# Out-projection of a hybrid mixer on one core: half the output columns in pairs of 512, with seven block products in place of eight for six of 16 tile pairs

## The chip, the core and the metric

The kernel runs on one core of a Trainium2 chip. The metric is the device time of one execution in microseconds. TensorE does matmuls of a 128x128 stationary operand with up to 512 moving columns and writes to eight banks of PSUM (128 partitions x 512 fp32). VectorE, ScalarE, GpSimd and SyncE each work through their own queue in order. Engines wait for each other through semaphores only.

## What is computed

One block of a hybrid sequence mixer, for x of 256 tokens x 4096. Cut to its frame:

```python
h = rms_norm(x, norm_g)
proj = h @ w_in                        # 256 x 4096 @ 4096 x N_IN
y_a = mLSTM heads of proj, chunked     # 1024 columns of y
y_b = sparse attention of proj         # 2048 columns
y_c = gated delta rule of proj         # 1024 columns
y = concatenate([y_a, y_b, y_c])       # 256 x 4096
out = x + y @ w_out                    # 256 x 4096 @ 4096 x 4096
```

The change is all in the last line, the out-projection. y holds 32 tiles of 128 rows of the contraction (kt 0 to 31); y_a is kt 0 to 7, y_b 8 to 23, y_c 24 to 31. Two neighbouring tiles, 2i and 2i+1, are called tile pair i here (i is 0 to 15).

## The kernel before

All weights are streamed once from HBM. The program cuts them into 536 chunks (`plan`), and every engine runs through the same list of chunks, each with its own part:

- SyncE loads chunk c into `w_raw[c % 4]`, 128 x 1024 fp32 (two tiles of the contraction x 512 columns), as soon as `w_lo` of chunk c-4 is made (`weights`).
- ScalarE writes `w_hi[c % 4]`, the same rounded to fp32r (`split_hi`, L1313), once TensorE is done with chunk c-4.
- VectorE writes `w_lo[c % 4]` = `w_raw` - `w_hi` (`split_lo`, L1650).
- TensorE (`chunk`, L1039, L1041, L1042) does three matmuls for each of two contraction tiles and two halves of the tokens: hi x hi, lo weights x hi operand, hi weights x lo operand. Twelve matmuls of 128x512 make a chunk. The operand is `op_hi` and `op_lo`, transposed tiles of h and later of y.

In the loops of ScalarE and VectorE, iteration c first handles the split of chunk c+3 (AHEAD is 3) and then the pieces woven into slot c: everything else of the mixer is cut into pieces with names of two or three letters, and `plan` writes by hand into which slot each goes. In the stretch that the change touches, these are `ae`, `ap`, `ay` (scores, product with v and norm of the mLSTM heads), `yd` and `yt` (blockwise turn of two tiles of y on VectorE, then `op_hi` on ScalarE and `op_lo` on VectorE), and `evac` (PSUM is added to x).

The out-projection is in 16 blocks. `out1` n (n from 0 to 7, chunks 408 to 503, twelve each) does kt 8 to 31 for output columns 512n and on, because y_a is not ready yet; `out2` n (chunks 504 to 535, four each) does kt 0 to 7. Both end in `evac`, which adds the two banks of 512 columns to `out_acc(n)`, first loaded with x. Even blocks use PSUM banks acc0, odd ones acc1; four more banks (mix) serve the woven pieces in turns. GpSimd loads x, moves blocks of y through HBM for the transposes and stores the finished columns. In slots 434 to 459 lie the last `ae`, `ap` and `ay`, the last `ay` in 459; `yd`/`yt` of tile pairs 0 to 3 lie in 469, 471, 473 and 475.

The order in ScalarE's and VectorE's loops:

```python
for c in range(len(chunks)):
    if c + AHEAD < len(chunks):
        split_lo(c + AHEAD)       # ScalarE: split_hi(c + AHEAD)
    for name, arg, use in woven[c]:
        pieces[name](arg, U0 + use)
```

`step(ins)` makes VectorE wait until its own instruction has ended, before it starts the next.

Of the kernel before, what the change touches and what calls it, by code (L numbers as in the profile page):

```python
# [13 lines left out]
F32 = mybir.dt.float32  # L14
# [88 lines left out]

USES = {"par": 2, "gt": 2, "gb": 1, "kx": 1, "cn": 1, "cg": 2, "cm": 1, "cu": 1,
# [4 lines left out]
def plan():  # L109
# [33 lines left out]
    for n in range(D // 512):  # L143
        block("out1", n, "y", full[kt_a:], wide, 512, "w_out", 512 * n)
    for n in range(D // 512):
        block("out2", n, "y", full[:kt_a], wide, 512, "w_out", 512 * n)

    chunks, last = [], []
    for b, blk in enumerate(blocks):
        for i in range(0, len(blk["kts"]), blk["per"]):  # L150
            chunks.append((b, blk["kts"][i:i + blk["per"]]))
        last.append(len(chunks) - 1)
# [18 lines left out]
    for b, x in enumerate(blocks):  # L171
        woven[last[b] if b else FIRST_EVAC].append(("evac", b))
# [50 lines left out]
    weave(first + 10, [("yt", i) for i in range(4, 16)])  # L223
    at = end("av", 1) + 2
# [5 lines left out]
    assert at <= end("out1", 7), (at, end("out1", 7))  # L230
# [10 lines left out]
def hybrid_kernel(nc, x, norm_g, w_in, w_out, m_ib, m_fb, m_norm_g, a_cq_g, a_wuq, a_wuqi, a_qn_g, a_kn_g,  # L241
# [13 lines left out]
    with ExitStack() as ctx:  # L255
# [6 lines left out]
        def region(names):  # L262

            with ExitStack() as stack:
# [14 lines left out]
                                       ("y_1", [P, D - 1024], F32), ("csq_lo", [P, 2, 512], F32R)])  # L279
        y = sb("y", [P, M, D])  # L280
        kv = sb("kv", [P, M, 1024])
# [7 lines left out]
        small = sb("small", [P, M, G_W])  # L289
        lane_u, lane_t = region([("lane_u", [P, BLK, LANE_C], F32), ("lane_t", [P, 320], F32)])  # L290
# [14 lines left out]

        xs, norm_in = region([("xs", [P, M, D], F32), ("norm_in", [P, P], F32)])
# [38 lines left out]
        def two_halves(v):  # L345
# [15 lines left out]
             ("a_h", [P, M, P], F32), ("a_sq", [P, P], F32), ("acc0", [P, M, W_A], F32)])  # L361

# [36 lines left out]
        rows_kept = sem("rows_kept")  # L399
        c_rows_ready = [sem(f"c_rows_ready{i}") for i in range(2)]  # L400
# [10 lines left out]
        conv_moved = [sem(f"conv_moved{i}") for i in range(2)]  # L411
# [37 lines left out]
        cq_moved = [sem(f"cq_moved{i}") for i in range(2)]  # L449
# [7 lines left out]
        bi_moved = [sem(f"bi_moved{i}") for i in range(2)]  # L457
# [5 lines left out]
        bq_moved = [sem(f"bq_moved{i}") for i in range(2)]  # L463
        bq_turned = sem("bq_turned")
        aqk_kept = sem("aqk_kept")
        aqk_moved = [sem(f"aqk_moved{i}") for i in range(2)]
# [6 lines left out]
        x_again = [sem(f"x_again{n}") for n in range(D // 512)]  # L473
        last_parts = sem("last_parts")
# [19 lines left out]

        def late_bank():
            return bank(U0 + uses)
# [157 lines left out]
        def _(sp):  # L654
# [5 lines left out]
            def weights(c):  # L660
                if c >= RAW_BUFS:
                    sp.wait_ge(lo_ready, c - RAW_BUFS + 1)
# [50 lines left out]
            for i, (m, n0, n1) in enumerate(LAST_PARTS):  # L713
                sp.wait_ge(last_out, i + 1)
                n = D - 512
# [6 lines left out]
        def _(pool):  # L722
# [68 lines left out]
            for j in range(6):  # L791
# [3 lines left out]
                bring_blocks(conv_stage(j), conv_dram[j % 2], conv_moved[j % 2])  # L795
# [108 lines left out]
            for i in range(2):  # L904
# [3 lines left out]
                bring_blocks(part, cq_dram[i], cq_moved[i])  # L908
# [6 lines left out]
            for j in range(2):  # L915
# [3 lines left out]
                bring_blocks(bi_in[j], bi_dram[j], bi_moved[j])  # L919
# [5 lines left out]
            def bring_queries(g):  # L925
# [4 lines left out]
                bring_blocks(two_halves(b_qT[:]), bq_dram[g], bq_moved[g % 2])  # L930
# [26 lines left out]
            def bring_aqk(j):  # L957

                pool.wait_ge(aqk_kept, 16 * 4 * M * (j + 1))
                bring_blocks(two_halves((a_qT, a_kT)[j][:]), aqk_dram[j], aqk_moved[j])  # L960
# [30 lines left out]
            for n in range(D // 512):  # L991
# [6 lines left out]
            for n in range(D // 512 - 1):  # L998
# [6 lines left out]
        def _(pe):  # L1005
# [6 lines left out]
            def chunk(c):  # L1012
# [3 lines left out]
                if kts[0] == blk["kts"][0] and b >= 2:  # L1016
# [5 lines left out]
                if c == len(chunks) - 1:  # L1022
                    wait_emptied(pe, U0 + uses)
# [4 lines left out]
                for i, kt, ms, n0, n1 in order:  # L1028
# [23 lines left out]
            pe_done = [0]  # L1052

# [236 lines left out]
        def _(act):  # L1290
# [906 lines left out]
```

## Time and profile before

| | us |
|---|---|
| median of 3 runs | 1540.96 |
| lowest, highest | 1540.08, 1541.07 |
| span of the profiled execution | 1538.2 |
| TensorE busy | 1533.7 |
| VectorE busy | 994.5 |
| ScalarE busy | 753.0 |
| GpSimd busy | 358.8 |

The span runs from the first to the last instruction of one profiled execution; the times of the runs also hold what lies around it. Matmuls are pipelined and the end of one is modelled, so two matmuls in a row overlap in the trace, and what one costs is read from the distance of starts. "Waited for" and "idle before" name the instruction that came last before the engine went on. PEclk is the granted clock of TensorE as a share of full speed.

### The profile page before, as it was taken

The numbers are of one execution on the slowest core, as the hardware profiler recorded it, in microseconds if no ns is written. First come the engines' busy times: TensorE is split into PE (matmuls) and PEld (weight loads), VectorE is DVE, ScalarE is ACT, GpSimd is POOL, SyncE is SP. The second block draws the span as 40 slices with busy tenths as digits, with TensorE's granted clock in tenths as the row PEclk, the third lists the DMA queues.
The fourth block names the chain that finished last, engine by engine and source line by source line (L and its number), as shares of the span: only waits on it lengthen the run. The fifth ranks groups of instructions, "written<-read, shape, count | busy, mean of one in ns | idle before, by whom it ended". The sixth has DMA issues, their size and how long they took to land.

```text
span 1538.2 us, 18847 instructions
## 1 busy us (share of the span) xinstructions
PE 1533.7 (100%) x6996; PEld 1270.8 (83%) x6996; DVE 994.5 (65%) x1537; ACT 753.0 (49%) x1006; POOL 358.8 (23%) x609
## 2 busy tenths in 40 slices
PE   9999999999999999999999999999999999999999
PEld 7888888888888888888878888888888888888887
DVE  6647555657759855676579667675456776664554
ACT  6745444587533444554545535535346444443332
POOL 9041112230230040127410354345300120200000
PEclk9999999999999999999999999999999999999999
DMA  9986778886787685568856787898885776666674
GB/s 285 292 244 196 220 213 230 204 244 190 223 242 214 196 223 159 166 182 267 250 176 194 219 244 216 228 274 249 255 250 178 249 221 192 208 198 194 196 246 156
DMA packets 206267, 337.77 MB, mean 220 GB/s; under 512 B 53049, under 2 KB 60520, under 8 KB 205920
## 3 DMA queue, kind: packets, MB, share of 16 engines
q1 hardware_dynamic: 184784, 288.66, 62.6%
q0 software_dynamic: 21344, 47.90, 11.8%
q8 instruction: 55, 0.90, 0.3%
q14 instruction: 36, 0.29, 0.1%
q10 hardware_dynamic: 48, 0.02, 0.0%
HBM read 312.81 MB, written 23.49 MB: 219 GB/s over the span
## 4 chain that ended last, share of the span: by engine, by line
PE 98%; DVE 1%; ACT 1%; issue 0%; DMA 0%; DVEq 0%
PE acc L1039 31%; PE acc L1042 31%; PE acc L1041 31%; PE mix L1102 1%; PE mix L1175 1%; PE mix L1164 0%; PE mix L1095 0%; PE acc L1243 0%; PE mix L1010 0%; DVE w_lo L1650 0%; ACT w_hi L1313 0%; PE mix L1161 0%; PE mix L1151 0%; PE mix L1149 0%; PE mix L1185 0%
## 5 line engine op out<-in xcount | busy, mean ns | idle before, releaser
L1650 DVE TENSOR_TENSOR w_lo<-w_raw,w_hi 128x1024 fp32r<-128x1024 f32 (+2 forms) x535 | 646.0, 1218 | 426.1 <-ACT w_hi L1313 422.6
L1313 ACT ACTIVATE w_hi<-w_raw 128x1024 fp32r<-128x1024 f32 (+2 forms) x535 | 556.3, 1050 | 536.3 <-PE acc L1042 434.1
L1039 PE MATMUL acc<-w_hi,op_hi 128*128 128x512 f32 (+1 forms) x2036 | 799.9, 393 | 0.3 <-DVE w_lo L1650 0.3
L1042 PE MATMUL acc<-w_hi,op_lo 128*128 128x512 f32 (+1 forms) x2036 | 792.9, 389 | 0.0
L1041 PE MATMUL acc<-w_lo,op_hi 128*128 128x512 f32 (+1 forms) x2036 | 791.9, 389 | 0.0
L1039 PEld LDWEIGHTS acc<-w_hi,op_hi 128*128 128x128 f32 x2036 | 382.5, 188 | 80.5 <-issue 1.9
L1042 PEld LDWEIGHTS acc<-w_hi,op_lo 128*128 128x128 f32 x2036 | 382.2, 188 | 80.1
L1041 PEld LDWEIGHTS acc<-w_lo,op_hi 128*128 128x128 f32 x2036 | 382.5, 188 | 77.7
L783 POOL DMA_DIRECT2D conv_dram<-y x48 | 30.7, 694 | 167.9 <-ACT y L1365 167.1
L783 POOL DMA_DIRECT2D y_dram<-y x32 | 20.5, 710 | 181.6 <-DVE y L2089 114.8
L937 POOL DMA_DIRECT2D bp_dram<-b_ps x48 | 31.5, 719 | 70.0 <-ACT b_ps L1534 67.0
L783 POOL DMA_DIRECT2D bq_dram<-qs x32 | 20.5, 715 | 76.4 <-DVE qs L1957 76.4
L1534 ACT ACTIVATE b_ps<-b_s,st 128x128 f32<-128x128 f32 (+1 forms) x32 | 14.3, 446 | 45.4 <-DVE st L2030 45.4
L948 POOL DMA_DIRECT2D b_pT<-bp_dram x48 | 26.5, 568 | 41.1 <-DMA bp_dram<-b_ps 41.0
L1039 PE MATMUL acc<-w_hi,cq_hi 128*128 128x512 f32 x84 | 33.5, 399 | 0.0
L1041 PE MATMUL acc<-w_lo,cq_hi 128*128 128x512 f32 x84 | 33.4, 397 | 0.0
L1042 PE MATMUL acc<-w_hi,cq_lo 128*128 128x512 f32 x84 | 33.1, 394 | 0.0
L789 POOL DMA_DIRECT2D y<-conv_dram x48 | 25.5, 541 | 23.5 <-DMA conv_dram<-y 23.4
L1000 POOL DMA_DIRECT2D out_dram<-acc x2 | 1.5, 729 | 125.8 <-DVE acc L1677 125.8
L1785 DVE SCALAR_TENSOR_TENSOR cT<-y,par,cT 128x255 f32<-128x255 f32 (+2 forms) x72 | 29.4, 478 | 0.0
L858 POOL DMA_DIRECT2D lane_out_dram<-lane_u x4 | 4.2, 1066 | 106.3 <-DVE lane_u L1846 106.3
L771 POOL DMA_DIRECT2D y<-in_x_dram x48 | 27.7, 585 | 0.0
(348 smaller groups left out, 974.2 us busy)
## 6 DMA issues: line engine op xcount, KB each, us to landing
w_raw<-in_w_in_dram SPq DMA_DIRECT2D x367, 512.0 KB, 4.7
w_raw<-in_w_out_dram SPq DMA_DIRECT2D x128, 512.0 KB, 4.5
w_raw<-in_w_in_dram SPq DMA_DIRECT2D x16, 384.0 KB, 3.3
w_raw<-in_a_wuq_dram SPq DMA_DIRECT2D x12, 512.0 KB, 5.4
conv_dram<-y POOLq DMA_DIRECT2D x48, 64.0 KB, 3.9
y<-conv_dram POOLq DMA_DIRECT2D x48, 64.0 KB, 4.7
w_raw<-in_a_wuqi_dram SPq DMA_DIRECT2D x6, 512.0 KB, 4.8
bp_dram<-b_ps POOLq DMA_DIRECT2D x48, 64.0 KB, 4.2
```

Source lines behind the costliest of these rows:

```text
L771: pool.dma_start(dst, src).then_inc(x_again[X_MOVED.index(c)], 16)
L783: pool.dma_start(*kept_block(dst, src, m, i)).then_inc(signal, 16)
L789: pool.dma_start(*moved_block(dst, src, q, j)).then_inc(signal, 16)
L937: pool.dma_start(bp_dram[n % 2][:, :, :, i, :].rearrange("a k j b -> a (k j) b"), b_ps[32 * i:32 * i + 32, n % 2].rearrange("p (f b) -> p ...
L948: pool.dma_start(b_pT[32 * j:32 * j + 32, n % 2], bp_dram[n % 2][:, :, j].rearrange("a k i b -> a k (i b)")).then_inc(bp_moved[n % 2], 16)
L1039: nc.tensor.matmul(o, hi[:, kt, tok], hv[:, i, n0:n1], start=(kt == (kts if late else blk["kts"])[0]), stop=False)
L1041: nc.tensor.matmul(o, hi[:, kt, tok], lv[:, i, n0:n1], start=False, stop=False)
L1042: last_mm = nc.tensor.matmul(o, lo[:, kt, tok], hv[:, i, n0:n1], start=False, stop=(kt == blk["kts"][-1]))
L1102: ins = nc.tensor.matmul(bank(use)[:, a * n:a * n + n], lhs(a), rhs(a), start=True, stop=True)
L1313: func(split_ap(w_hi, c), w_raw[:, c % RAW_BUFS, 0:n], ACT.Copy).then_inc(hi_ready, 1)
L1650: vec.tensor_tensor(split_ap(w_lo, c), w_raw[:, c % RAW_BUFS, 0:n], split_ap(w_hi, c).bitcast(F32), ALU.subtract).then_inc(lo_ready, 1)
L1785: ins = vec.scalar_tensor_tensor(cT[:, c, d:SEQ], conv_columns(i, j)[:, 0:SEQ - d], par[:, row:row + 1], cT[:, c, d:SEQ], ALU.mult, ALU.add)
```

## The change

Output columns 0 to 2047 stay as they are: `out1` and `out2` for n from 0 to 3. Columns 2048 to 4095 become two column pairs (n = 4 and 5, n = 6 and 7). A column pair goes once over all 16 tile pairs, in the order of PAIR_KTS, with the two column blocks' chunks in turn. It stands between `out1` 3 and `out2` 0: chunks 456 to 487 and 488 to 519. Four banks collect its four sums (two token halves x two column blocks): the acc banks for the first column pair, the mix banks for the second.

For tile pairs 8 to 13 (SEVEN) the 2x2 blocks of operand and of weights are multiplied by Strassen's scheme in Winograd's form, seven products in place of eight, each again of three matmuls. The chunk of the first column block (`seven_first`) has two products (6 matmuls), that of the second (`seven_second`) five (15 matmuls). Four products go to four more banks.

- Sums over y are made once: `ss` (VectorE, four operations of 128x128, then ScalarE, 512 columns rounded) and `sl` (VectorE, 512 columns), in slots 434, 437, ... 449 and 435, 438, ... 450.
- Sums over the weights are made for each of the 12 chunks of a second column block: VectorE makes `t_raw` (4 x 512) in three operations with a wait after the first and the second, within `split_lo`; ScalarE rounds it to `t_hi` (2048 columns), within `split_hi`, behind the rounding of the one raw block still wanted; VectorE makes `t_lo` (2048 columns) in `seven_lo`, which stands behind `split_lo` of the next chunk. There is one buffer of each.
- In the order of chunks a seven takes two, and two plain chunks lie between two sevens; in the first column pair the second chunks of the sevens are 461, 465, 469, 473, 477 and 481. Of `seven_second`'s five products the first reads only raw weights' splits, the other four read `t_hi` and `t_lo`.
- `evs` recombines the four banks of the Strassen products into the sums with x (one ScalarE copy, eight VectorE operations), behind the last seven of a column pair; `evn` adds the four plain banks at its end.
- `w_raw` of a first chunk is kept until the sums of the second are made. Some semaphores are merged into `brought` to stay within their number. Loads of x and stores of out move in GpSimd's queue.

```diff
+OUT_SINGLE = 4
+PAIR_KTS = [14, 15, 8, 4, 9, 5, 10, 6, 11, 7, 12, 0, 13, 1, 2, 3]
+SEVEN = [8, 9, 10, 11, 12, 13]
...
+    for n in range(OUT_SINGLE, D // 512):
+        block("pair", n, "y", [2 * i + j for i in PAIR_KTS for j in range(2)], wide, 512, "w_out", 512 * n)
...
+    weave(first + 26, [("ss", i) for i in SEVEN], 3)
+    weave(first + 27, [("sl", i) for i in SEVEN], 3)
...
             def weights(c):
                 if c >= RAW_BUFS:
-                    sp.wait_ge(lo_ready, c - RAW_BUFS + 1)
+                    d = c - RAW_BUFS
+                    sp.wait_ge(lo_ready, d + 2 if in_seven(d) and not second_col(d) else d + 1)
...
+            def three(o, x_hi, x_lo, w_hi_, w_lo_, start, stop):
+                nc.tensor.matmul(o, x_hi, w_hi_, start=start, stop=False)
+                nc.tensor.matmul(o, x_hi, w_lo_, start=False, stop=False)
+                return nc.tensor.matmul(o, x_lo, w_hi_, start=False, stop=stop)
...
+            def seven_first(c):
...
+                three(seven_banks(p)[0], op_hi[:, 2 * i, tok], op_lo[:, 2 * i, tok], hv[:, 0], lv[:, 0],
+                      i == SEVEN[0], i == SEVEN[-1])
+                three(plain_banks(p)[0], op_hi[:, 2 * i + 1, tok], op_lo[:, 2 * i + 1, tok], hv[:, 1], lv[:, 1],
+                      False, False).then_inc(split_used, 1)
...
+            def seven_second(c):
...
+                pe.wait_ge(lo_ready, c + 1)
...
+                three(c12, *s4, hv[:, 1], lv[:, 1], False, False)
+                pe.wait_ge(t_lo_ready, sevens.index(c) + 1)
+                three(c21, *a22, t_hi[:, 3], t_lo[:, 3], False, False)
+                three(p5, *s1, t_hi[:, 0], t_lo[:, 0], first, end_)
+                three(p6, *s2, t_hi[:, 2], t_lo[:, 2], first, end_)
+                three(p7, *s3, t_hi[:, 1], t_lo[:, 1], first, end_).then_inc(split_used, 1)
...
             def split_hi(c):
                 act.wait_ge(raw_ready[c % RAW_BUFS], raw_count(c))
                 if c >= SPLIT_BUFS:
...
+                    wait_used(act, c - SPLIT_BUFS)
...
+                if in_seven(c) and second_col(c):
+                    func(w_hi[:, c % SPLIT_BUFS, 512:1024], w_raw[:, c % RAW_BUFS, 512:1024], ACT.Copy
+                         ).then_inc(hi_ready, 1)
+                    act.wait_ge(t_summed, sevens.index(c) + 1)
+                    if c > sevens[0]:
+                        wait_used(act, sevens[sevens.index(c) - 1])
+                    func(t_hi[:], t_raw[:], ACT.Copy).then_inc(t_hi_ready, 1)
+                    return
...
             def split_lo(c):
                 dve.wait_ge(hi_ready, c + 1)
+                if in_seven(c) and second_col(c):
...
+                    step(vec.tensor_tensor(t_raw[:, 0:2], w_raw[:, b0 + 1].rearrange("p (k n) -> p k n", k=2),
+                                           w_raw[:, b0:b0 + 2, 0:512], ALU.subtract))
+                    step(vec.tensor_tensor(t_raw[:, 2], b22, t_raw[:, 0], ALU.subtract))
+                    vec.tensor_tensor(t_raw[:, 3], w_raw[:, b0, 512:1024], t_raw[:, 2], ALU.subtract
+                                      ).then_inc(t_summed, 1)
+                    vec.tensor_tensor(w_lo[:, c % SPLIT_BUFS, 512:1024], b22,
+                                      w_hi[:, c % SPLIT_BUFS, 512:1024].bitcast(F32), ALU.subtract
+                                      ).then_inc(lo_ready, 1)
+                    return
...
+            def seven_lo(c):
+
+                n = sevens.index(c)
+                dve.wait_ge(t_hi_ready, n + 1)
+                vec.tensor_tensor(t_lo[:], t_raw[:], t_hi[:].bitcast(F32), ALU.subtract).then_inc(t_lo_ready, 1)
...
+            def ss(i, use):
+                a11, a21, a12, a22 = [y_columns(i)[:, P * j:P * j + P] for j in range(4)]
+                step(vec.tensor_tensor(a22, a21, a22, ALU.add))
+                step(vec.tensor_tensor(a21, a11, a21, ALU.subtract))
+                step(vec.tensor_tensor(a11, a22, a11, ALU.subtract))
+                vec.tensor_tensor(a12, a12, a11, ALU.subtract).then_inc(s_summed, 1)
...
                 if c + AHEAD < len(chunks):
                     split_lo(c + AHEAD)
+                if c + AHEAD - 1 in sevens:
+                    seven_lo(c + AHEAD - 1)
```

## Rows read from the trace of the kernel before

**Rows 1.** The page: span, busy time of each engine, chain that ended last by engine.
```profile
span 1538.2 us, 18847 instructions
...
PE 1533.7 (100%) x6996; PEld 1270.8 (83%) x6996; DVE 994.5 (65%) x1537; ACT 753.0 (49%) x1006; POOL 358.8 (23%) x609
...
PE 98%; DVE 1%; ACT 1%; issue 0%; DMA 0%; DVEq 0%
```
**Rows 2.** What TensorE waited for: line, releaser, us in total, times, longest.
```profile
PE mix L1250 <- DVE kv L2139: 1.1, 1, 1.1
PE acc L1039 <- DVE w_lo L1650: 0.3, 1, 0.3
```
**Rows 3.** Timeline, two chunks of an `out1` block: start, duration, engine, instruction, idle before.
```profile
1401.79 0.39 PE L1042 MATMUL acc<-w_hi,op_lo 128*128 128x512 f32 x1
...
1402.01 0.39 PE L1039 MATMUL acc<-w_hi,op_hi 128*128 128x512 f32 x1
...
1402.27 1.06 ACT L1313 ACTIVATE w_hi<-w_raw 128x1024 fp32r<-128x1024 f32 x1 [1.66 <-PE acc L1042]
...
1403.37 1.23 DVE L1650 TENSOR_TENSOR w_lo<-w_raw,w_hi 128x1024 fp32r<-128x1024 f32 x1 [1.49 <-ACT w_hi L1313]
...
1404.73 0.39 PE L1039 MATMUL acc<-w_hi,op_hi 128*128 128x512 f32 x1
```
**Rows 4.** Groups by shape, whole run: the splits of 1024 columns (busy us, mean ns).
```profile
L1650 DVE TENSOR_TENSOR w_lo<-w_raw,w_hi 128x1024 fp32r<-128x1024 f32 x513 | 623.1, 1225 | 405.9 <-ACT w_hi L1313 402.6
L1313 ACT ACTIVATE w_hi<-w_raw 128x1024 fp32r<-128x1024 f32 x513 | 536.8, 1056 | 523.5 <-PE acc L1042 429.7 <-DMA w_raw<-in_w_in_dram 85.9 <-DMA w_raw<-in_w_out_dram 7.4
```
**Rows 5.** Groups by shape, whole run: 512 columns on VectorE and ScalarE.
```profile
L1361 ACT ACTIVATE qs<-acc 128x512 f32<-128x512 f32 x10 | 6.0, 597 | 1.4 <-PE acc L1042 1.0 <-issue 0.2
L1650 DVE TENSOR_TENSOR w_lo<-w_raw,w_hi 128x512 fp32r<-128x512 f32 x6 | 4.1, 689 | 4.0 <-ACT w_hi L1313 3.8
L1313 ACT ACTIVATE w_hi<-w_raw 128x512 fp32r<-128x512 f32 x6 | 3.7, 622 | 0.0
```
**Rows 6.** Timeline near 1309 us: two splits back to back on an engine.
```profile
1308.54 1.99 ACT L1313 ACTIVATE w_hi<-w_raw 128x1024 fp32r<-128x1024 f32 x2
...
1309.62 2.36 DVE L1650 TENSOR_TENSOR w_lo<-w_raw,w_hi 128x1024 fp32r<-128x1024 f32 x2 [1.85 <-ACT w_hi L1313]
```
**Rows 7.** Timeline near 10 us: TensorE starts again behind VectorE.
```profile
9.20 0.88 DVE L2131 SCALAR_TENSOR_TENSOR op_lo<-mix,par,op_hi 128x256 fp32r<-128x256 f32 x2 [1.43 <-ACT op_hi L1579]
...
10.23 0.30 PEld L1243 LDWEIGHTS acc<-w_hi,op_hi 128*128 128x128 f32 x2 [0.35 <-DVE op_lo L2131]
10.26 0.47 PE L1243 MATMUL acc<-w_hi,op_hi 128*128 128x512 f32 x1
```
**Rows 8.** DMA issues: count, KB each, median us from issue to landing.
```profile
w_raw<-in_w_out_dram SPq DMA_DIRECT2D x128, 512.0 KB, 4.5
```
**Rows 9.** VectorE's timeline: first instruction of an `ay` and the split behind it.
```profile
1290.44 0.16 DVE L1696 TENSOR_SCALAR st<-st 128x2 f32<-128x2 f32 x1
...
1293.26 1.22 DVE L1650 TENSOR_TENSOR w_lo<-w_raw,w_hi 128x1024 fp32r<-128x1024 f32 x1
```
**Rows 10.** Groups by shape, whole run: `yd`, `yt` on both engines, a 128-wide operation.
```profile
L2098 DVE STREAM_TRANSPOSE y<-y 128x512 f32<-128x512 f32 x16 | 11.3, 704 | 0.0
L1564 ACT ACTIVATE op_hi<-y,par 128x256 fp32r<-128x256 f32 x16 | 7.2, 498 | 7.7 <-DVE y L2098 7.7
L2110 DVE SCALAR_TENSOR_TENSOR op_lo<-y,par,op_hi 128x256 fp32r<-128x256 f32 x16 | 7.0, 479 | 3.9 <-ACT op_hi L1564 3.9
...
L2014 DVE TENSOR_TENSOR sc<-sc,low 128x128 f32<-128x128 f32 x2 | 0.6, 292 | 0.1
```
**Rows 11.** Busy us by stretch: PE, PEld, DVE, ACT, POOL; PEclk, DMA share, GB/s.
```profile
1255.00:1300.00 45.00, 45.00 (x212) 36.81 (x211) 32.04 (x67) 19.85 (x31) 9.40 (x16) 1.00 0.68 209
20.00:1538.00 1518.00, 1515.20 (x6912) 1255.54 (x6910) 983.05 (x1519) 741.41 (x987) 340.73 (x565) 1.00 0.75 218
```

More of the change, by code:

```diff
@@ L149, in plan @@
     for b, blk in enumerate(blocks):
+        second = blk["kind"] == "pair" and blk["arg"] % 2
+        if second:
+            last.append(len(chunks) - 1)
+            last[b - 1] = last[b] - 1
+            continue
         for i in range(0, len(blk["kts"]), blk["per"]):
-            chunks.append((b, blk["kts"][i:i + blk["per"]]))
+            for q in range(2 if blk["kind"] == "pair" else 1):
+                chunks.append((b + q, blk["kts"][i:i + blk["per"]]))
         last.append(len(chunks) - 1)
@@ L171, in plan @@
     for b, x in enumerate(blocks):
-        woven[last[b] if b else FIRST_EVAC].append(("evac", b))
+        if x["kind"] != "pair":
+            woven[last[b] if b else FIRST_EVAC].append(("evac", b))
+        elif x["arg"] % 2:
+            of_seven = [c for c, (b_, kts) in enumerate(chunks) if b_ == b and kts[0] // 2 in SEVEN]
+            woven[of_seven[-1]].append(("evs", x["arg"] // 2 - OUT_SINGLE // 2))
+            woven[last[b]].append(("evn", x["arg"] // 2 - OUT_SINGLE // 2))
     woven[NX - 1].append(("par", 0))
@@ L229, in plan @@
     at = weave(at + 8, [[("yd", i), ("yt", i)] for i in range(4)], 2)
-    assert at <= end("out1", 7), (at, end("out1", 7))
+    first_a = next(c for c, (b, kts) in enumerate(chunks) if blocks[b]["kind"] == "pair" and kts[0] == 0)
+    assert at <= first_a, (at, first_a)
     use, order = 0, {}
@@ new lines, in seven_second @@
+            def seven_second(c):
+                p, i = pair_of(c), chunks[c][1][0] // 2
+                pe.wait_ge(lo_ready, c + 1)
+                hv = split_ap(w_hi, c).rearrange("p (k n) -> p k n", k=2)
+                lv = split_ap(w_lo, c).rearrange("p (k n) -> p k n", k=2)
+                s2, s3, s4, s1 = [(s_hi(i)[:, P * j:P * j + P], s_lo(i)[:, P * j:P * j + P]) for j in range(4)]
+                tok = slice(P, 2 * P)
+                a22 = op_hi[:, 2 * i + 1, tok], op_lo[:, 2 * i + 1, tok]
+                _, p5, p6, p7 = seven_banks(p)
+                _, c21, c12, _ = plain_banks(p)
+                first, end_ = i == SEVEN[0], i == SEVEN[-1]
+                three(c12, *s4, hv[:, 1], lv[:, 1], False, False)
[4 more added lines that the diff above has]
+                three(p7, *s3, t_hi[:, 1], t_lo[:, 1], first, end_).then_inc(split_used, 1)
@@ new lines, in evn @@
+            def evn(p, use):
+                b = pair_block(p)
+                for k in range(4):
+                    if k % 2 == 0:
+                        dve.wait_ge(acc_ready, b + 1 + k // 2)
+                    dst = pair_sum(p)[:, k % 2, 512 * (k // 2):512 * (k // 2) + 512]
+                    ins = vec.tensor_tensor(dst, plain_banks(p)[k], dst, ALU.add)
+                    if p == 1:
+                        done_bank(ins, four_mix(1)[k])
+                    elif k % 2:
+                        ins.then_inc(acc_read[k // 2], 1)
+                    else:
+                        step(ins)
```

196 lines of the change are left out of this document (163 added, 33 removed).

## The prediction

> **What bounds the kernel now.** The page comes first [rows 1]: TensorE is busy in 1533.7 of 1538.2 us and 98% of the chain that ended last is TensorE's, nearly all of it in the three matmul lines of `chunk`. The list of what TensorE waited for is a few rows, 1.1 us the longest [rows 2]. So every matmul lies on the path, and the other engines count only where they make TensorE wait. A chunk is twelve 128x512 matmuls; the timeline [rows 3] has the same point of two neighbouring chunks at 1402.01 and 1404.73, so a chunk takes 2.72 us and a matmul 0.227 us (the 0.39 us shown for one overlap the next). VectorE with 65% and ScalarE with 49% look as if they had room. Those are averages; what matters below is how long a chain across them takes.
>
> How that chain stands today is in the same rows. Let T be the moment at which TensorE goes on from chunk d to d+1 (1402.01). ScalarE starts `w_hi` of chunk d+4 at T + 0.26 (the buffer of d is free), VectorE starts its `w_lo` 1.10 us later, at T + 1.36, and is done at T + 2.59. TensorE wants it at T + 3 x 2.72 = T + 8.16. The slack is 5.6 us per chunk. It is this that the change spends.
>
> **What is removed.** For each of six tile pairs in each of two column pairs, 24 matmuls become 21 (seven products of three, where eight were): 12 x 3 = 36 matmuls, 36 x 0.227 = 8.2 us off the path. There is no other removal; the chunks stay 536, and the bytes of weights the same. "Seven" below is such a tile pair; its chunks are s-1 (first column block, 6 matmuls, 1.36 us) and s (second, 15 matmuls, 3.40 us). Between two sevens lie two plain chunks, so the period is four chunks, 10.88 us today and 45 x 0.227 = 10.20 us if nothing waits.
>
> **What is added at each seven, step by step.** At s the four weight sums have to be made, split into high and low, and only then can twelve of its fifteen matmuls run (the first three need only the raw block). Durations: ScalarE takes 1.06 us for 1024 columns and 0.62 for 512 [rows 4, 5], 0.43 us more for 512 more, so 1.93 for `t_hi` (2048). VectorE takes 1.22 for 1024 and 0.69 for 512 [rows 4, 5], so 2.30 for `t_lo`. Between engines 0.04 us pass, from TensorE's last matmul 0.09 [rows 3]; two operations back to back on one engine overlap by some 0.1 us, their pairs taking 1.99 and 2.36 us [rows 6]. With T the end of chunk s-4:
> - ScalarE: `w_hi` of s, 512 columns, T+0.26 to 0.88.
> - VectorE: the sum over 1024 columns to 2.14, then the two over 512, each waiting for the one before: to 3.60. Nothing overlaps here, because each `step` waits.
> - ScalarE: `t_hi`, 3.64 to 5.57. It sits inside `split_hi(s)`, so what is queued behind it is `w_hi` of chunk s+1: in place of T+2.98 it starts at 5.44 and ends at 6.50.
> - VectorE: in its order `split_lo(s+1)` stands ahead of `seven_lo(s)`. So `w_lo` of s+1 runs from 6.54, and `t_lo` from 7.67 to 9.97.
> - TensorE: two plain chunks and s-1 take it to T+6.80, its first three matmuls of s to 7.48. Then it waits for `t_lo`. After a wait the first weight load starts 0.15 us and the first matmul 0.18 us after the releaser, and that matmul takes 0.08 longer [rows 7]: 10.23. Twelve matmuls more: 12.95.
>
> The wait is 2.75 us, and as s is the s-4 of the next seven, this is a closed loop: 12.95 us in place of 10.88, **2.07 us lost per seven** after the matmuls saved. The first seven of a column pair starts from the same T with the same chain. Twelve times: **+24.8 us**. Bounds: with no hop at all and `t_lo` at 2 us the wait would be some 2.1 us (+17 us in sum); with every hop doubled and half a microsecond of delay of `w_hi` of s+1 it is 3.5 (+34).
>
> Does anything else bind in the loop? Weights: the buffer of s-1 is now kept until the sums are made, so two transfers are issued at about T+4.3; a transfer lands in 4.5 us [rows 8], the second some 2 us later, at 9 and 11. They are wanted at T+7.06 and T+13.2, and TensorE only comes to the first of them behind the wait. Nothing is added. VectorE's work in a period is 1.2 + 1.2 + 1.2 for the three full splits, 2.6 for sums, 0.6 and 2.2, together 9.0 of 12.95 us: it fits, and there would be room even in 10.2.
>
> **Pieces that share the queues.** In the first column pair four pieces `yd`/`yt` and one `ay` are woven among the sevens. Where one stands behind `t_lo` or behind the split of s+3, VectorE comes late to the next sums, which it could start at T+13.87 (0.92 behind 12.95). `ay` takes 2.82 us, from 1290.44 to the next split at 1293.26 [rows 9]: 9.97 + 2.82 + two splits of 1.13 and 1.23 = 15.1, +1.2. A `yd`/`yt` is a turn of 0.70 on VectorE, two `op_hi` of about 0.9 on ScalarE and two `op_lo` of about 0.9 on VectorE, one after another [rows 10]: 2.5 us. The first comes behind a split at 12.2, giving +0.9; the second and third fall into one loop (9.97 + 2.5 + 2.4 + 2.5 = 17.3), +3.4; the fourth +1.0. Sum **+6.5 us**, bounds 0 (all in idle time) and 12 (each in full).
>
> **Sums over y.** Six `ss` and six `sl` are put between chunks 434 and 450, each some 1.3 us (four 128-wide operations of 0.29 and their waits) and 0.7 us of VectorE [rows 5, 10]: 12 us. In the 45 us from 1255 to 1300 it has 32.0 us of work already [rows 11], so it comes to 44 of 45, with an order in which ScalarE and VectorE wait for each other twice per `ss`. The slack of 5.6 us takes most of it; at the `ae` of chunk 448, counting on from the evacuation at 443, the splits of 452 and 453 come some 0.5 and 1.4 us late. I take **+2 us**, bounds 0 and 6.
>
> **At no cost.** The Strassen products are evacuated by one ScalarE copy (0.60 [rows 5]) and eight VectorE operations of 0.6 to 0.73: behind the last seven's end they take VectorE from 0.90 to 6.2, the next split is done at 7.5, TensorE wants it at 8.16. The cover is three plain chunks; without them up to 5 us would show, twice. `evn` (four operations, 2.9 us) has the cover of `evac`. Loads of x and stores of out move on GpSimd's queue into the middle of the run; 0.5 MB lands in 4 to 5 us [rows 8] and nobody comes for it sooner. Merged semaphores change no wait's time. The tail is the same code.
>
> **Sum.** The times shown are 1540.08 to 1541.07, median 1540.96; the profiled span is 1538.2, 2.8 us less, and I let those 2.8 us stand. 1540.96 + 24.8 + 6.5 + 2 = 1574.3 us.
>
> **Rivals.**
> - *The chain is hidden and the saving stands.* 1540.96 - 8.2 = 1532.8. For it: 65% and 49% busy engines, 5.6 us of slack. Against it: `t_lo` would have to be there at T+7.48, 2.5 us sooner than rows of these very lines allow. It takes a faster pass over 2048 columns than any row shows, or an order that isn't the code's. 0.09.
> - *The chain shows only in part*, net near nothing: 0.03. The turning point is a wait of 0.68 us per seven.
> - *Only the loop costs*; y's sums and the woven pieces fall into idle time: 1540.96 + 24.8 = 1565.8. 0.25.
> - *The forecast*, 1574.3: 0.45.
> - *The pieces cost more*, each in full, with late weights besides: 24.8 + 12 + 6 and some 6 more, about 1590. 0.12.
> - *The clock falls behind the waits.* The granted clock is 1.00 in every stretch, which is 2.4 GHz [rows 11], but TensorE never waits longer than 1.1 us there [rows 2], so no row tells what 2.75 us would do. At half the clock (1.2 GHz) the twelve matmuls behind each wait take 2.72 us more: 1574.3 + 12 x 2.72 = 1607. 0.06. [...]
> - *The change doesn't do what it says.* The code issues 21 matmuls per seven; the count has to fall from 6996 to 6960. I give this nothing of its own.
>
> **How the numbers follow.** The likeliest case gives 1574.3. The range reaches from 1558 (the loop's lower bound with nothing more) to 1594 (pieces in full) and holds the three middle cases, 0.82. What a measurement can tell from no change is about 0.2%, 3 us. Faster 0.09, within 0.2% 0.03, slower 0.88.
>
> **What would show it.** 6960 matmuls. TensorE waiting twelve times on the line of `t_lo`, some 2.7 us each and 33 in sum, longer (4 to 6 us) at two or three places in the first column pair, and hardly there on `w_lo`. ScalarE's `w_hi` of s+1 starting at once behind `t_hi`, VectorE idle between `w_lo` of s and of s+1. Distance between ends of sevens near 12.95 in the second column pair. A few microseconds of waits on `w_lo` between chunks 448 and 454. What would make it wrong: a 2048-wide operation at another price per column, weights landing late now that two start together, or the clock.

## The result and the profile after

| | before | after |
|---|---|---|
| median | 1541.01 us (1540.08 to 1541.35, 4 runs) | 1585.86 us (1583.7 to 1589.02, 4 runs) |
| ratio | | 1.0292, 95% interval 1.028 to 1.0304 |
| span of the profiled execution | 1538.2 | 1587.3 |

The change makes the kernel 44.9 us slower. The profiled execution of the changed kernel is the slowest of its four (1589.0 us, with a mean granted clock of 0.989 where the others have 0.991 or 0.992), so its trace shows 3 us more than the median, and sums read from it are held against the trace.

A remark on the text ahead of the prediction: it puts the sums over y (`ss`, `sl`) into slots 434 to 450. That is 16 slots too late; `first` in `plan` is 392, not 408, and they stand in 418 to 434, from 1211 to 1255 us in the trace of after. The load of VectorE there (1210 to 1255 us of the old trace) is 32.5 of 45 us, much as the 32.0 of [rows 11].

The page of the changed kernel, the lines that answer to [rows 1]:
```profile
span 1587.3 us, 18905 instructions
...
PE 1546.2 (97%) x6960; PEld 1274.4 (80%) x6960; DVE 1056.0 (67%) x1623; ACT 772.6 (49%) x1026; POOL 357.7 (23%) x609
...
PE 86%; DVE 8%; ACT 3%; issue 2%; DMA 1%; ACTq 0%; DVEq 0%
```
The matmuls are down by 36, as promised, and TensorE is busy for 12.5 us longer all the same: some of its matmuls have become slower. 14% of the chain that ended last is not TensorE's now (8% VectorE, 3% ScalarE, the rest issue and DMA). What TensorE waits for, where [rows 2] had 1.4 us:
```profile
PE acc L1179 <- DVE t_lo L1850: 17.8, 6, 4.2
PE mix L1179 <- DVE t_lo L1850: 14.3, 6, 2.6
PE acc L1163 <- DVE w_lo L1843: 4.4, 5, 1.8
```
Twelve waits for `t_lo`, one per seven ("acc" is the first column pair, "mix" the second), and four new ones for `w_lo` (4.1 us; the fifth of the row stands before the change's stretch), all between 1226 and 1259 us, where the sums over y stand.

What those sums cost in all is read from matmuls that are the same in both kernels, number 5601 and number 5761 of TensorE's, around that stretch. Before, then after:
```profile
1225.51 0.39 PE L1039 MATMUL acc<-w_hi,op_hi 128*128 128x512 f32 x1
1259.70 0.40 PE L1042 MATMUL acc<-w_hi,op_lo 128*128 128x512 f32 x1
```
```profile
1224.75 0.39 PE L1163 MATMUL acc<-w_hi,op_hi 128*128 128x512 f32 x1
...
1242.36 0.50 PE L1163 MATMUL acc<-w_hi,op_hi 128*128 128x512 f32 x1 [1.85 <-DVE w_lo L1843]
...
1266.46 0.40 PE L1166 MATMUL acc<-w_hi,op_lo 128*128 128x512 f32 x1
```
34.2 us have become 41.7: 7.5 us lost here, more than the waits alone show, because restarts and one stretch of slow matmuls (below) come on top.

The first seven of the second column pair, all engines (start, duration, instruction, idle before):
```profile
1441.09 0.63 ACT L1478 ACTIVATE w_hi<-w_raw 128x512 fp32r<-128x512 f32 x1 [1.94 <-PE mix L1166]
...
1441.75 1.23 DVE L1833 TENSOR_TENSOR t_raw<-w_raw 128x1024 f32<-128x1024 f32 x1 [1.34 <-ACT w_hi L1478]
1443.01 0.69 DVE L1835 TENSOR_TENSOR t_raw<-w_raw,t_raw 128x512 f32<-128x512 f32 x1
1443.74 0.69 DVE L1836 TENSOR_TENSOR t_raw<-w_raw,t_raw 128x512 f32<-128x512 f32 x1
...
1444.46 1.92 ACT L1483 ACTIVATE t_hi<-t_raw 128x2048 fp32r<-128x2048 f32 x1 [2.74 <-DVE t_raw L1836]
1446.29 1.99 ACT L1485 ACTIVATE w_hi<-w_raw 128x1024 fp32r<-128x1024 f32 x2
...
1447.36 1.23 DVE L1843 TENSOR_TENSOR w_lo<-w_raw,w_hi 128x1024 fp32r<-128x1024 f32 x1 [2.33 <-ACT w_hi L1485]
1448.50 2.28 DVE L1850 TENSOR_TENSOR t_lo<-t_raw,t_hi 128x2048 fp32r<-128x2048 f32 x1
...
1450.84 0.50 PE L1179 MATMUL mix<-t_hi,op_hi 128*128 128x512 f32 x1 [2.65 <-DVE t_lo L1850]
...
1452.30 0.63 PE L1181 MATMUL acc<-t_hi,s_even 128*128 128x512 f32 x1
...
1455.28 0.39 PE L1163 MATMUL mix<-w_hi,op_hi 128*128 128x512 f32 x1
```
Counted back 0.26 us from ScalarE's start, as in the prediction, T is 1440.83, and `t_lo` ends at 1450.78, T + 9.95. (TensorE itself went on at 1440.55; ScalarE came 0.28 us late to this first seven. In the next one TensorE goes on at 1455.28 and the first product with t starts at 1465.29, 10.01 us later, as in all loops after it.) ScalarE starts `w_hi` of the next chunk right behind `t_hi`, and VectorE sits idle for 2.33 us before that chunk's `w_lo`, which stands ahead of `t_lo`. Then comes what the chain of steps doesn't explain: from the fifth matmul behind the wait on, eight stand 0.42 or 0.43 us apart and not 0.227, and the twelve take 4.44 us. The same stretch by windows (PE, PEld, DVE, ACT, POOL; then granted clock, DMA share, GB/s):
```profile
1441.00:1447.00 6.00, 6.00 (x28) 4.98 (x27) 3.21 (x4) 3.17 (x3) 0.00 (x0) 1.00 0.47 145
1448.30:1450.80 2.50, 0.00 (x0) 0.00 (x0) 2.50 (x3) 1.06 (x1) 0.00 (x0) 1.00 0.84 271
1451.90:1455.20 3.30, 3.30 (x9) 2.61 (x8) 1.16 (x2) 0.00 (x0) 0.00 (x0) 0.50 0.56 159
1455.40:1461.00 5.60, 5.60 (x27) 4.58 (x26) 3.21 (x4) 2.72 (x3) 0.00 (x0) 1.00 0.08 14
```
The granted clock is 0.50 (1.2 GHz) for the stretch behind the wait and back at 1.00 after it. The trace has ten such stretches of seven or eight slow matmuls: nine behind waits for `t_lo`, one behind the wait of 1.85 us for `w_lo` at 1242 us. They don't follow every wait: behind those at 1340.88 (3.38 us idle), 1479.74 (2.35) and 1507.10 (2.33) the matmuls run at full clock.

### The profile page after: what moved, and what is told of

Read it like the earlier page. It is cut to its first block, busy times and chain, and to the rows that moved or that the text cites. A ratio compares the mean times of both kernels' runs of the same rounds, so it can differ in the third digit from the quotient of the medians.

```text
span 1587.3 us, 18905 instructions
## 1 busy us (share of the span) xinstructions
PE 1546.2 (97%) x6960; PEld 1274.4 (80%) x6960; DVE 1056.0 (67%) x1623; ACT 772.6 (49%) x1026; POOL 357.7 (23%) x609
## 3 DMA queue, kind: packets, MB, share of 16 engines
q0 software_dynamic: 21344, 47.90, 11.3%
## 4 chain that ended last, share of the span: by engine, by line
PE 86%; DVE 8%; ACT 3%; issue 2%; DMA 1%; ACTq 0%; DVEq 0%
PE acc L1163 26%; PE acc L1166 25%; PE acc L1165 25%; DVE w_lo L1843 3%; ACT w_hi L1485 2%; DVE t_lo L1850 2%; PE mix L1271 1%; DVE t_raw L1833 1%; PE mix L1344 1%; DMA w_raw<-in_w_out_dram 1%; PE mix L1163 1%; PE mix L1165 1%; PE mix L1166 1%; PE mix L1179 1%; PE acc L1179 1%
## 5 line engine op out<-in xcount | busy, mean ns | idle before, releaser
L1163 PE MATMUL acc<-w_hi,op_hi 128*128 128x512 f32 (+1 forms) x1860 | 733.0, 394 | 4.5 <-DVE w_lo L1843 4.4
L1166 PE MATMUL acc<-w_hi,op_lo 128*128 128x512 f32 (+1 forms) x1860 | 724.6, 390 | 0.0
L1165 PE MATMUL acc<-w_lo,op_hi 128*128 128x512 f32 (+1 forms) x1860 | 724.3, 389 | 0.0
L1163 PEld LDWEIGHTS acc<-w_hi,op_hi 128*128 128x128 f32 x1860 | 349.9, 188 | 79.1 <-DVE w_lo L1843 7.1
L1166 PEld LDWEIGHTS acc<-w_hi,op_lo 128*128 128x128 f32 x1860 | 349.5, 188 | 74.2
L1165 PEld LDWEIGHTS acc<-w_lo,op_hi 128*128 128x128 f32 x1860 | 349.9, 188 | 71.0
L1483 ACT ACTIVATE t_hi<-t_raw 128x2048 fp32r<-128x2048 f32 x12 | 23.0, 1918 | 34.9 <-DVE t_raw L1836 34.9
L1706 ACT ACTIVATE b_ps<-b_s,st 128x128 f32<-128x128 f32 (+1 forms) x32 | 14.3, 446 | 45.8 <-DVE st L2290 45.8
L1163 PE MATMUL mix<-w_hi,op_hi 128*128 128x512 f32 (+1 forms) x82 | 31.8, 387 | 0.0
L1166 PE MATMUL mix<-w_hi,op_lo 128*128 128x512 f32 (+1 forms) x82 | 31.8, 387 | 0.0
L1165 PE MATMUL mix<-w_lo,op_hi 128*128 128x512 f32 (+1 forms) x82 | 31.7, 387 | 0.0
```

Source lines behind the costliest of these rows:

```text
L1163: nc.tensor.matmul(o, hi[:, kt, tok], hv[:, i, n0:n1], start=(kt == (kts if late else blk["kts"])[0]), stop=False)
L1165: nc.tensor.matmul(o, hi[:, kt, tok], lv[:, i, n0:n1], start=False, stop=False)
L1166: last_mm = nc.tensor.matmul(o, lo[:, kt, tok], hv[:, i, n0:n1], start=False, stop=(kt == blk["kts"][-1]))
L1483: func(t_hi[:], t_raw[:], ACT.Copy).then_inc(t_hi_ready, 1)
```

## The experiments

Theory A, as in the prediction with what the trace added: a chain of dependent steps makes TensorE wait at each seven, and behind such a wait the clock often falls. Theory B: VectorE simply has too much work there. Theory C: products that read `t_hi` and `t_lo` are slow of themselves.

### One line moved: `t_lo` ahead of the next split

```diff
-                if c + AHEAD < len(chunks):
-                    split_lo(c + AHEAD)
                 if c + AHEAD - 1 in sevens:
                     seven_lo(c + AHEAD - 1)
+                if c + AHEAD < len(chunks):
+                    split_lo(c + AHEAD)
```


> One change to the changed kernel: in VectorE's loop seven_lo(s) stands ahead of split_lo(s+1), not behind it. Same instructions, same bytes. Theory A (the wait is a chain of dependent steps, and the clock falls behind the waits): t_lo needn't wait for w_hi and w_lo of chunk s+1 any more and ends 2.1 us sooner, at T+7.9 where the changed kernel has T+9.95 (T is the end of chunk s-4). TensorE's twelve waits on t_lo fall from 32.1 us in sum to 5 to 10, the stretches at 1.2 GHz behind them become fewer than the nine there are; time about 1551 us (1544 to 1560). Theory B (VectorE has too much work in the column pairs, 9.0 us in 10.2): order alone changes nothing in the sum of work, the time stays at 1580 or more. Theory C (the four products read t_hi and t_lo slowly, whatever comes before): the waits go but the slow matmuls stay, 7 or 8 of them in nine sevens: about 1565.

Measured: 1558.19 us (1557.97 to 1559.51), ratio 1.0111 (1.0095 to 1.0127). The time lies within what was expected (1544 to 1560), above its middle of 1551. Two statements in another order are worth 27.7 us. What TensorE waited for:
```profile
PE acc L1179 <- DVE t_lo L1850: 9.8, 6, 2.7
PE acc L1163 <- DVE w_lo L1843: 3.9, 4, 1.8
PE acc L1179 <- DVE w_lo L1838: 2.2, 2, 1.8
PE mix L1179 <- DVE t_lo L1850: 1.9, 6, 0.6
```
In the second column pair 14.3 us of waits are 1.9, a loop takes 10.84 us, and no slow stretch is left there. Products that read t stand 0.233 us apart where the others have 0.227, not 0.43, so theory C falls as an account of the slow stretches. The first column pair keeps 12.0 us and two slow stretches, and the waits sum to 13.9 us where 5 to 10 were expected: there the order of the chain isn't all.

### The sums over weights one chunk sooner

```diff
             def split_lo(c):
                 dve.wait_ge(hi_ready, c + 1)
                 if in_seven(c) and second_col(c):
-                    ... three sums into t_raw
...
+                    seven_lo(c)
                     return
...
+            def seven_sums(c):
+                dve.wait_ge(raw_ready[c % RAW_BUFS], raw_count(c))
+                if c > sevens[0]:
+                    dve.wait_ge(t_lo_ready, sevens.index(c))
+                ... the same three sums
...
                 if c + AHEAD < len(chunks):
                     split_lo(c + AHEAD)
-                if c + AHEAD - 1 in sevens:
-                    seven_lo(c + AHEAD - 1)
+                if c + AHEAD + 1 in sevens:
+                    seven_sums(c + AHEAD + 1)
```


> One change to the changed kernel: the three sums over weights are made one chunk sooner, behind split_lo(s-1), as soon as the raw weights are there, and t_hi then only waits for TensorE's end of chunk s-4; t_lo stands behind w_lo of s, ahead of the next split. Same instructions, same bytes. Theory A: t_hi runs from T+0.8 to T+2.7, t_lo to T+5.1, 2.4 us before TensorE wants it at T+7.5. No waits on t_lo, at most one or two where pieces are woven in, no slow stretch in the column pairs; the 8.2 us of the 36 matmuls show, and what is left is the stretch of the sums over y (4.1 us of waits on w_lo and one slow stretch): 1541 - 8.2 + 7 = 1540 us (1535 to 1546), against 1586 of the changed kernel. Theory B (too much work for VectorE): 1575 or more, with waits on w_lo or t_lo all along the column pairs. Theory C: slow matmuls stay in the sevens, 1555.

Measured: 1553.88 us (1552.73 to 1555.08), ratio 1.0081 (1.0066 to 1.0097). Expected were 1535 to 1546, so this missed by some 8 us. In the second column pair nothing waits any more, and sevens follow each other every 10.30 us. In the first one the waits stayed, two slow stretches among them:
```profile
PE acc L1179 <- DVE t_lo L1858: 8.9, 5, 2.5
PE acc L1163 <- DVE w_lo L1838: 5.6, 6, 1.8
PE acc L1179 <- DVE w_lo L1832: 1.3, 2, 1.0
```
VectorE between two sevens of the first column pair, with one `yd`/`yt` behind the sums and one behind a split:
```profile
1368.63 0.69 DVE L1850 TENSOR_TENSOR t_raw<-w_raw,t_raw 128x512 f32<-128x512 f32 x1
1369.36 0.69 DVE L1851 TENSOR_TENSOR t_raw<-w_raw,t_raw 128x512 f32<-128x512 f32 x1
1369.97 0.70 DVE L2366 STREAM_TRANSPOSE y<-y 128x512 f32<-128x512 f32 x1
1371.65 0.88 DVE L2378 SCALAR_TENSOR_TENSOR op_lo<-y,par,op_hi 128x256 fp32r<-128x256 f32 x2 [0.98 <-ACT op_hi L1736]
1372.45 0.68 DVE L1832 TENSOR_TENSOR w_lo<-w_raw,w_hi 128x512 fp32r<-128x512 f32 x1
1373.97 2.29 DVE L1858 TENSOR_TENSOR t_lo<-t_raw,t_hi 128x2048 fp32r<-128x2048 f32 x1 [0.84 <-ACT t_hi L1483]
```
Here theory B has a part, but not all of it. A loop holds about 9 us of VectorE's work and has 10.3 us; with the pieces, this one (1365.2 to 1380.7) holds 11.5 us, more than a loop of 10.3 has room for. But it took 15.5 us, and VectorE stood idle in 4.0 of them, nearly all of it for ScalarE: 1.1 us for a `w_hi`, 0.98 us for `op_hi`, twice, and 0.84 us for `t_hi`, which ScalarE started only behind the first of these `op_hi` and the `w_hi` of 512 columns. So a piece costs its own work and also lengthens the chain, because it stands ahead of `t_hi` in ScalarE's queue and ahead of `w_lo` and `t_lo` in VectorE's. No run here separates the two.

### Zero products in the wait

```diff
+FILL = 10
...
+            step(nc.gpsimd.memset(zeros[:].bitcast(F32), 0.0))
...
                 three(c12, *s4, hv[:, 1], lv[:, 1], False, False)
+                pe.wait_ge(const_ready, 2)
+                for _ in range(FILL):
+                    nc.tensor.matmul(c12, zeros[:], hv[:, 1], start=False, stop=False)
                 pe.wait_ge(t_lo_ready, sevens.index(c) + 1)
```


> The changed kernel with ten more matmuls of 128x512 per seven, put in front of TensorE's wait for t_lo: a zero operand times w_hi, added into a sum, so 2.27 us of matmuls without effect in a wait of 2.3 to 4.2 us. 120 matmuls more. Theory A with the clock as a cause of its own: t_lo comes as late as before, so TensorE goes on at the same points of the chain, but the clock has no reason to fall; the waits on t_lo shrink to 5 to 12 us in sum, the nine slow stretches in the column pairs go or nearly, each worth 8 matmuls x 0.2 = 1.6 us: 1586 - 14 = 1572 us (1568 to 1577), faster with more matmuls. Theory C (the products with t_hi and t_lo are slow of themselves): slow stretches stay, time 1586. If TensorE's order costs more than thought: 1590 or more.

Measured: 1578.61 us (1576.9 to 1580.6), ratio 1.0242 (1.0226 to 1.0258): 7.3 us faster than the changed kernel, with 120 matmuls more (expected 1568 to 1577, so the gain was smaller than forecast). `t_lo` comes when it came, and TensorE goes on at the same point of the loop, but the clock holds:
```profile
1458.99 2.43 PE L1222 MATMUL mix<-w_hi,zeros 128*128 128x512 f32 x10
1461.50 0.50 PE L1182 MATMUL mix<-t_hi,op_hi 128*128 128x512 f32 x1
1461.83 0.40 PE L1183 MATMUL mix<-t_lo,op_hi 128*128 128x512 f32 x1
```
One slow stretch is left of ten. In the second column pair the first product with t starts every 12.91 or 12.92 us in all five intervals, where the changed kernel has 14.45, 14.45, 12.91, 14.45 and 12.92. So a slow stretch costs 1.53 us there. In the first column pair it may cost nothing: the interval from 1383.58 to 1399.91 of the changed kernel is 16.33 us with a slow stretch in it, and the one of this kernel is 16.33 without: VectorE is what comes last there. And where the clock holds in the stretch of the sums over y, TensorE runs ahead and waits longer (5.6 us on `w_lo` in place of 4.4): between the same two matmuls 7.4 us are lost here and 7.5 in the changed kernel, so the slow stretch cost nothing there. That is why it is 7.3 us and not the 14 I had expected: ten times 1.6 was too simple a sum.

### The sums made only once

```diff
-                pe.wait_ge(t_lo_ready, sevens.index(c) + 1)
+                pe.wait_ge(t_lo_ready, 1)
...
-                    act.wait_ge(t_summed, sevens.index(c) + 1)
                     if c > sevens[0]:
-                        wait_used(act, sevens[sevens.index(c) - 1])
+                        return
+                    act.wait_ge(t_summed, 1)
                     func(t_hi[:], t_raw[:], ACT.Copy).then_inc(t_hi_ready, 1)
...
+                    if c > sevens[0]:
+                        ... w_lo of the raw block alone
+                        return
...
-                if c + AHEAD - 1 in sevens:
+                if c + AHEAD - 1 == sevens[0]:
```


> The changed kernel with t_raw, t_hi and t_lo made for the first seven only; the other eleven multiply with that old t. Left out: eleven times the three sums, the rounding and the split of t (output differs for that reason). TensorE's instructions are all there, 36 fewer than before. It measures the saving by itself. Theory A: one wait on t_lo (3.4 us and a slow stretch), the sums over y as before (4.1 us of waits and one slow stretch of 1.6): 1541 - 8.2 + 3.5 + 4.1 + 2 x 1.6 + restarts of 1 = 1545 us (1540 to 1549). Theory B: the same or less. Theory C: the products read t tiles that nobody writes; if reading from there is slow, slow matmuls stay in the sevens and it is 1560. If the order of blocks and banks in pairs costs by itself, it shows here as what is above 1549.

Measured: 1544.36 us (1543.24 to 1544.98), ratio 1.0021 (1.0011 to 1.0031), as expected (1545). Where no t is made there is no wait, and a loop takes 10.30 us. From it the saving is read: 10.88 - 10.30 = 0.58 us per seven, 7.0 us in all, where I had 0.68 and 8.2. Most of the missing 0.10 us shows in the distances of starts: the twelve products that read `t_hi` or `t_lo` stand 0.233 us apart, here and in every other kernel with sevens, and all others 0.227, which makes 0.08 us per seven. Why these are 3% slower no run tells.

### Seven products in the second column pair only

```diff
-            return blocks[b]["kind"] == "pair" and kts[0] // 2 in SEVEN
+            return blocks[b]["kind"] == "pair" and blocks[b]["arg"] >= 6 and kts[0] // 2 in SEVEN
...
-    weave(first + 26, [("ss", i) for i in SEVEN], 3)
-    weave(first + 27, [("sl", i) for i in SEVEN], 3)
+    for i, at in zip(SEVEN, SUM_AT):       # SUM_AT = [68, 70, 72, 74, 85, 87]
+        weave(first + at, [("ss", i), ("sl", i)])
```
with the order of the second experiment; the first column pair runs plainly.

> The order of e2 (sums over weights one chunk sooner), with seven products only in the second column pair; the first takes all its tile pairs plainly. The six sums over y are made in slots 460, 462, 464, 466, 477 and 479, where no piece of the mixer is left but yd/yt in 469 to 475, in place of 418 to 434 among the pieces of the heads. 18 matmuls fewer than before the change, 18 x 0.227 = 4.1 us. Theory A (VectorE's and ScalarE's queue decide where a seven can be had for nothing: in e2 the second column pair shows no wait at all, all 16 us of waits are where other pieces are woven in): no wait of TensorE on t_lo or w_lo, no stretch at 1.2 GHz, 1540.9 - 4.1 = 1536.8 us (1535.5 to 1539), faster than the kernel before. Theory B (a column pair costs something by itself, in banks, loads of x or stores): 1541 or more with no wait in the trace that explains it.

Measured: 1536.32 us (1534.48 to 1537.21), ratio 0.9972 (0.9962 to 0.9982). It is faster than both kernels, by 3.9 us against the one before (1540.22 in the same runs), and within what was expected. The profile lists no wait of TensorE behind 976 us; its longest ones, all up to there:
```profile
PE mix L1420 <- DVE kv L2411: 1.1, 1, 1.1
PE mix L1331 <- issue: 0.4, 1, 0.4
PE acc L1391 <- ACT w_hi L1780: 0.4, 1, 0.4
```
So neither the column pairs nor their banks, loads and stores cost anything that shows, and between the two matmuls around 1225 and 1260 us, where the sums over y have been taken away, nothing is lost (0.05 us).

### The sums over y spread out

The second experiment with `ss` and `sl` in slots 423, 426, 436, 439, 444 and 452, each `sl` one behind.

```diff
-    weave(first + 26, [("ss", i) for i in SEVEN], 3)
-    weave(first + 27, [("sl", i) for i in SEVEN], 3)
+    for i, at in zip(SEVEN, SUM_AT):       # SUM_AT = [31, 34, 44, 47, 52, 60]
+        weave(first + at, [("ss", i), ("sl", i)])
```


> e2 with the six sums over y (ss and sl) spread over slots 423 to 452, into slots where no other piece stands, in place of every third slot from 418 on. All else as e2, whose TensorE waits 4.9 us on w_lo between 1230 and 1260 us. Theory A (local backlog on VectorE, and ScalarE and VectorE waiting for each other): these waits go, the waits of the first column pair stay at about 10 us; e2's 1553.9 - 5 - 0.5 = 1548 us (1546 to 1550.5). Theory B (VectorE is full over the whole stretch of the heads, so that spreading only moves the waits): 1552 to 1555.

Measured: 1551.66 us (1551.33 to 1553.37), ratio 1.0076 (1.0061 to 1.0092). 2.2 us less than the second experiment, between the two theories:
```profile
PE acc L1180 <- DVE t_lo L1859: 8.1, 4, 2.5
PE acc L1164 <- DVE y L1930: 2.3, 1, 2.3
PE acc L1180 <- DVE w_lo L1833: 1.8, 1, 1.8
PE acc L1164 <- DVE w_lo L1839: 1.4, 2, 1.1
```
The waits at 1230 to 1260 us are gone, but one of 1.1 us stands at 1293 and one of 2.3 us at 1323, behind VectorE's late `evac`. Spread out, the same work still isn't free among the heads' pieces (4.4 us are lost ahead of the first seven, where the second experiment lost 6.6); in the experiment above, behind the heads, it costs nothing.

### The chain alone, and filled

The faster kernel (seven products in the second column pair only), with the changed kernel's order of sums, `t_hi` and `t_lo` put back (the second experiment's diff taken back); and the same with ten zero products ahead of each wait.

> e5 (seven products in the second column pair only, sums over y in free slots) with the order of the changed kernel put back: sums within split_lo(s), t_hi behind them, t_lo behind split_lo(s+1). The chain is the only thing that differs from e5, and no other piece is woven there. Theory A: six loops of 12.92 us where e5 has 10.20, so 6 x 2.72 = 16.3 us of waiting, and the clock falls behind some four of six waits as it did in the changed kernel's second column pair, 1.53 us each (a loop of 14.45 in place of 12.92): 1536.3 + 16.3 + 6.1 = 1559 us (1556 to 1562). If the chain's price depends on what else is woven in (theory B), the waits come out other than 2.3 us each and the time below 1552 or above 1565.

> e8 with ten matmuls of a zero operand ahead of each of the six waits on t_lo, 60 more in all, as in e3. It measures the clock's share alone: the loops stay at 12.92 us because t_lo comes when it comes, and no stretch at 1.2 GHz is left. Theory A with the clock as a second cause: e8 less 1.53 us for each of its slow loops, 1552.8 us (1551 to 1555), 3 to 9 us below e8. If the slow stretches were of no account (TensorE would wait for VectorE all the same): the same time as e8.

Measured: 1554.26 us (1553.44 to 1555.16), ratio 1.0087 (1.0073 to 1.0101); filled 1551.46 us (1550.56 to 1552.19), ratio 1.007 (1.0056 to 1.0084). The chain alone:
```profile
PE mix L1181 <- DVE t_lo L1851: 14.1, 6, 2.4
...
1431.51 0.50 PE L1181 MATMUL mix<-t_hi,op_hi 128*128 128x512 f32 x1 [2.35 <-DVE t_lo L1851]
...
1444.43 0.79 PE L1181 MATMUL mix<-t_hi,op_hi 128*128 128x512 f32 x1 [2.33 <-DVE t_lo L1851]
...
1458.73 0.50 PE L1181 MATMUL mix<-t_hi,op_hi 128*128 128x512 f32 x1 [2.33 <-DVE t_lo L1851]
```
The loops are 12.92 us, and 14.30 and 14.34 where the clock falls (the row of 0.79 us is a slow matmul). 1554.26 lies below the expected 1556 to 1562. Of the 4.7 us to its middle 3.3 are the clock, which fell behind two of six waits and not behind four, and 0.6 are the loops without the chain, which take 10.30 us and not 10.20. Filled, it came within what was expected, and all five intervals are 12.91 or 12.92. So the chain costs 6 x (12.92 - 10.30) = 15.7 us for six sevens (expected 16.3); the medians give 1551.46 - 1536.32 = 15.1. The clock costs another 2.8 for two stretches. Waits of one length and one spacing had four slow stretches behind them in the changed kernel's second column pair and two here: how many come can't be told from the waits.

## Why the prediction was right, and which step was not

I forecast 1574.3 us in 1558 to 1594 and slower with 0.88. It is 1585.9. The sign and the main cause hold; one cause I had put aside is in the result, and one term was far too small. The terms are read from the traces. In that of the changed kernel the last matmul starts 49.05 us later than before, though at 1225 us, ahead of all that was changed, it was 0.8 us early by chance; what was added behind is 49.8. In the kernel with zero products, where the clock holds but for one stretch, the last matmul is 40.65 us late, and 0.6 of it by chance. The profiled executions are 2 to 3 us above the medians of their kernels, so the terms don't add up to 44.9.

- **The loop.** Forecast 12.95 us, `t_lo` ended at T+9.97, a wait of 2.75. Measured 12.92 and T+9.95, and the first product with t starts 2.53 us later than it could (T+10.01 for T+7.48); the idle time of 2.33 us in the list counts from the modelled end of the last matmul. The 2048-wide steps, which no row showed, took 1.92 and 2.28 us against 1.93 and 2.30. Two small errors cancel: the restart costs 0.17 us and not 0.26, and the twelve products with t take 2.80 and not 2.72. 12 x (12.92 - 10.88) = 24.5 us, forecast 24.8. The mechanism is right; one line moved undoes most of it.
- **The saving.** 7.0 us and not 8.2, but the sum above compares loops and is not touched by it.
- **Pieces in the first column pair.** Forecast 6.5, measured 6.6 with the clock held (zero products), in part by luck. There the intervals of the first column pair are 14.03, 12.92, 13.70, 16.33 and 14.46 us, the last with a slow stretch of about 1.5. Above 12.92 that is 1.1 for `ay` (forecast 1.2), then 0, then 0.8 and 3.4 for `yd`/`yt` (forecast 0.9 and 3.4), and 0 for the fourth (forecast 1.0). The other 1.3 are at a place that I had put at nothing, "the same T with the same chain": the first seven of the first column pair came 1.0 us late, because the last `ap`, woven into slot 456, keeps ScalarE until 1329.7 us, so that `w_hi` and `w_lo` of chunk 460, behind which the sums stand, come late (with no piece there, in the chain alone, `t_lo` of the first seven ends at T+9.96 like the others); the first of the second column pair came 0.3 late, and why is open.
- **Sums over y.** Forecast 2 with bounds of 0 and 6, at a place that was 16 slots off. Measured 7.5 us between the two matmuls around them, 7.4 with the clock held, and nothing when the sums stand behind the heads. This term of the sum was mis-sized, and outside its bounds: four waits of 0.3 to 1.85 us, with their restarts, are in it where I had counted splits that come 0.5 and 1.4 us late at one place and a slack that takes most of it.
- **The clock.** This is the step that failed. I left it out of the sum and gave it 0.06 as a rival. It fell ten times. 24.5 + 6.6 + 7.4 makes 38.5 us; of the 49.8 us 11.3 are left, and these are the clock's, all in the column pairs. The run with zero products bears it out: 38.5, its one slow stretch of 1.5 and the 0.6 make 40.6 of its 40.65. My price for the rival, twelve matmuls at half the clock behind each wait (+32.6 us, 1607), was wrong too: 7 or 8 matmuls are slow, 1.4 to 1.5 us, and only where nothing else is late. I argued that no row showed a wait of this length, and took that for a reason to leave it out; it was a reason to put one end of the range there. That the range held the time it owes to the width given for the pieces: without the clock, 38.5 us would have given about 1579. The Trainium skill, TensorE: Matmul & The Clock Gate, section "Why this matters for your kernels", has the rule that idle gaps between bursts of matmuls, beyond a length that it names, send the array to half rate. The trace agrees as to the fall and not as to the length: eight of the ten falls stand behind waits shorter than the page's (1.85 to 2.65 us), and behind one of 3.38 us, which is longer, there was none.
- **At no cost.** TensorE has no wait behind `evs` or `evn` in the trace of after (from the last seven to the end the distance to the old trace grows by 0.04 us), and none in the kernel with seven products in the second column pair only, so that was right, the loads and stores too, the 0.3 us above left open.

## What to carry to other kernels

Where one engine is full and the others look half idle, count the longest chain of dependent steps between "buffer free" and "operand wanted", with every instruction that stands ahead in each in-order queue, and compare it with the slack (here 9.95 us against 7.5); that gave the loop to 0.03 us, where the busy shares said there was room. A matmul saved is worth 0.23 us, so the operations that buy it must find both a place in the order and room in the sum of work: the same arithmetic was 2.9% slower or 0.8% slower by placement alone, and half of it, well placed, 0.3% faster. And a wait of TensorE of 2 us can have a second price behind it, the slow clock, which belongs into the range from the start.

## What the runs showed of the hardware

- In the changed kernel the granted clock fell from 1.00 (2.4 GHz) to 0.50 (1.2 GHz) behind waits of TensorE of 1.85 us (once) and 2.1 to 4.2 us, for seven or eight matmuls of 128x512 at a distance of 0.43 us. Of its twelve waits for `t_lo` nine had such a stretch behind them, of the six in the kernel with the chain alone two, and a wait of 1.86 us at the same place in the kernel with zero products had none.
- With ten zero products in each of six waits (the last run) it is 1.00 from 1410 to 1535 us, where the same waits left empty had two falls behind them.
- 120 matmuls that compute nothing made the kernel 7.3 us faster.
- Matmuls of 128x512 whose moving operand is `t_hi` or `t_lo` stand 0.233 us apart, the others 0.227.
- A 2048-wide fp32 operation of two inputs takes 2.28 us on VectorE, a 2048-wide copy to fp32r 1.92 us on ScalarE, each in line with its own 512 and 1024.
